# Neighbourhood attention of a fused four-block network: pairs of heads on TensorE side by side, values token-major

## The reference, cut to what matters

```
q = _heads(hx, w[:, :hd], na_q_g[j])            # RMS norm over each head
k = _heads(hx, w[:, hd:2 * hd], na_k_g[j])
v = _heads(hx, w[:, 2 * hd:])
k_c = _heads(hc, w[:, hd:2 * hd], na_k_g[j])    # 256 context tokens
v_c = _heads(hc, w[:, 2 * hd:])
...
    bias = jnp.take(bias_cols, row_off, axis=1)
    s_loc = jnp.einsum('bwhd,brwchd->bhwrc', q_r, k_win).astype(jnp.float32) * scale
...
x = x + gx1 * (_neighbourhood_attention(q, k, v, k_c, v_c, na_rpb[j]) @ na_w_out[j])
```

## Time and profile before

| | us |
|---|---|
| median of 3 runs | 3102.87 (3100.97 to 3104.98) |
| the profiled execution, its own time | 3100.61 |
| its span, first to last instruction | 3098.8 |
| from the start of `na_v` to the first turned numerators | 107.12 |
| the 64 attention steps | 153.28 |
| from the last of them to the first matmul of `res2` | 5.64 |
| PE busy, share of the span | 93% |
| granted TensorE clock, mean | 0.966 |

### The profile page before, as it was taken

The page is one execution under the profiler, slowest core; times in us unless marked ns, Lnnn a source line. Parts: engine busy times, 40 slices in busy tenths (PEclk is TensorE's granted clock), DMA queues, the critical chain, the costliest instruction groups (busy, mean ns, idle before and its releaser), DMA issues.

```text
span 3098.8 us, 39305 instructions
## 1 busy us (share of the span) xinstructions
PE 2885.5 (93%) x14018; PEld 2347.0 (76%) x14018; DVE 1626.7 (52%) x2371; ACT 1133.8 (37%) x1857; POOL 1090.1 (35%) x501
## 2 busy tenths in 40 slices
PE   4998899998998899997999799999979989989999
PEld 3885588886776578874878688888858878868887
DVE  6537696854456788855222416655542565431111
ACT  3333443334464533235112413121243357542222
POOL 2440444445322444443212123232323233234443
PEclk9999899998999899998999899999979989999999
DMA  5351355532421355531211123333312110122222
GB/s 209 122 181 34 119 187 203 190 109 79 158 69 65 108 185 193 178 109 42 68 68 48 41 82 115 130 133 121 126 61 67 50 42 22 36 76 98 95 95 88
DMA packets 90419, 325.47 MB, mean 105 GB/s; under 512 B 10036, under 2 KB 12852, under 8 KB 89784
## 3 DMA queue, kind: packets, MB, share of 16 engines
q1 hardware_dynamic: 85392, 312.21, 29.5%
q10 hardware_dynamic: 4904, 11.68, 1.2%
HBM read 321.75 MB, written 2.10 MB: 105 GB/s over the span
## 4 chain that ended last, share of the span: by engine, by line
PE 84%; DVE 8%; ACT 4%; issue 2%; DMA 1%; POOL 1%; DVEq 0%; ACTq 0%; SPq 0%; POOLq 0%
PE bank L1293 58%; PE junk L1295 9%; PE bank L1076 2%; PE bank L1221 2%; PE bank L1061 1%; PE bank L1208 1%; PE bank L1310 1%; PE bank L1200 1%; PE bank L1180 1%; PE junk L1200 1%; ACT UF L816 1%; ACT Uh L816 1%; PE bank L1102 1%; DVE ADA L1383 1%; DMA ADA<-in_ast 1%
## 5 line engine op out<-in xcount | busy, mean ns | idle before, releaser
L466 POOL TENSOR_TENSOR WL<-RAW,WH 128x1024 fp32r<-128x1024 f32 x392 | 979.1, 2499 | 1784.4 <-ACT WH L760 1276.7
L760 ACT ACTIVATE WH<-RAW 128x1024 fp32r<-128x1024 f32 x292 | 307.2, 1052 | 381.9 <-PE junk L1295 188.1
L1293 PE MATMUL bank<-U1h,WH 128*128 128x512 f32 x960 | 378.1, 394 | 18.0 <-DVE U1l L1631 17.8
L1293 PE MATMUL bank<-Uh,WH 128*128 128x512 f32 x832 | 341.2, 410 | 55.5 <-DVE Ul L1633 54.9
L1293 PE MATMUL bank<-U1l,WH 128*128 128x512 f32 x960 | 375.5, 391 | 0.0
L1293 PE MATMUL bank<-U1h,WL 128*128 128x512 f32 x960 | 375.4, 391 | 0.0
L1293 PE MATMUL bank<-Hh,WH 128*128 128x512 f32 x864 | 340.2, 394 | 11.7 <-DVE Hl L548 11.7
L1293 PE MATMUL bank<-Hl,WH 128*128 128x512 f32 x864 | 339.0, 392 | 0.0
L1293 PE MATMUL bank<-Hh,WL 128*128 128x512 f32 x864 | 338.8, 392 | 0.0
L1293 PE MATMUL bank<-Ul,WH 128*128 128x512 f32 x832 | 331.5, 398 | 0.0
L1293 PE MATMUL bank<-Uh,WL 128*128 128x512 f32 x832 | 331.2, 398 | 0.0
(11 more groups left out here) (334 smaller groups left out, 5249.3 us busy)
## 6 DMA issues: line engine op xcount, KB each, us to landing
RAW<-in_wst SPq DMA_DIRECT2D x392, 512.0 KB, 3.4
ADA<-in_ast SPq DMA_DIRECT2D x192, 512.0 KB, 4.5
NST<-in_nstrip ACTq DMA_DIRECT2D x16, 192.0 KB, 2.3
XT<-in_xt SPq DMA_DIRECT2D x1, 2048.0 KB, 15.4
STRIP<-in_strip ACTq DMA_DIRECT2D x8, 256.0 KB, 2.6
CB<-in_cb ACTq DMA_DIRECT2D x4, 512.0 KB, 4.2
DX<-in_dx ACTq DMA_DIRECT2D x1, 2048.0 KB, 8.3
out_xt<-XT SPq DMA_DIRECT2D x1, 2048.0 KB, 6.2
```

Source lines behind the costliest of these rows:

```text
L466: pool.tensor_tensor(WL[:, s4], RAW[:, s2], WH[:, s4].bitcast(F32), ALU.subtract)\
L760: act.activation(WH[:, c % 4], RAW[:, c % 2], ACT.Copy).then_inc(S("hi_done"), 1)
L1293: mm = pe.matmul(bank_of(p, u)[:], w[:, u, k], x[:, k, 0:T], start=st and m == 0, stop=en and m == 2)
```

## The change

1. Attention goes by pairs of heads: 32 steps i = 4t + b, for head pair t and query block b. Scores are three passes of two matmuls, head 2t from partitions 0 to 63 and head 2t+1 from 64 to 127, each 512 columns wide (256 context and 256 grid keys in one bank). Values are the stationary operand, 64 channels wide, and the turned numerators move: the two heads write partitions 0 to 63 and 64 to 127 of bank 4. The result has channels on partitions, so `turn_out` goes.
2. The division: the sums are spread over 64 columns each by a reciprocal into RB (`roots`), PE turns RB into bank 5 by eight f32 matmuls for each t (`spread`), ACT copies it to RX, DVE multiplies bank 4 by RX into OF (`out_of`), ACT and POOL split OF into OHN and OLN. The order of tokens changes there from grid columns to rows.
3. Masked biases come from memory, 768 KB for each t (`load_bias`), where POOL added mask and bias. Bias and maximum are one DVE instruction for each head (`na_logits`), 512 wide; ACT no longer copies context scores. Of the turned numerators ACT copies one head, DVE the other.
4. The high half of the keys is made by DVE (`key_hi`, was ACT).
5. The values are projected token-major (`na_values_pe`): tokens stationary, weights moving, 8 jobs in two halves of 512 channels, six banks for 768 tokens. `v_turn` goes; ACT and DVE copy three banks each at the end of a half, and two DMAs for each half make the copies of VN shifted by 64 tokens. The head norm of `na_k` tiles stays beside the jobs. The scores of step 0 are put ahead of the last bank's matmuls.
6. The norm ahead of the block writes its tokens by grid column (DVE, the branch k == 2), so ACT writes QN and KN without the reordering.

The diff, cut to its core (left out: POOL's loop that now only makes low halves, ACT's side with the same roles as described, layouts, semaphores' names, and the host's preparation):

```diff
-    add("na_v", 8, 3, "u", 48, ctx=True)
+    add("na_v", 8, 3, "u", 48)
...
+        NA_S = ((6, 7), (0, 1))
...
+                def low(t):
+                    pool.wait_ge(S("n_qhi"), t + 1)
+                    pool.wait_ge(S("n_khi"), t + 1)
+                    pool.tensor_tensor(QNl[:, t], QN[:, t], QNh[:, t % 2].bitcast(F32), ALU.subtract)
+                    pool.tensor_tensor(KNl[:, t * TC:(t + 1) * TC], KN[:, t], KNh[:, t % 2 * TC:(t % 2 + 1) * TC].bitcast(F32),
+                                       ALU.subtract).then_inc(S("n_lo"), 1)
+                def out_low(t):
+                    pool.wait_ge(S("o_hi"), 16 + t + 1)
+                    pool.tensor_tensor(OLN[:, t, 0:T], OF[:, t % 2], OHN[:, t].bitcast(F32), ALU.subtract).then_inc(S("o_ready"), 1)
+                pool.wait_ge(S("pe_job"), N_V + 5)
+                pool.memset(NB[:, 0:C], 0.0).then_inc(S("n_zero"), 1)
+                low(0)
+                for t in range(KT):
+                    if t + 1 < KT:
+                        low(t + 1)
+                    if t >= 1:
+                        out_low(t - 1)
...
+        def na_scores(pe, i):
+            t, b = divmod(i, 4)
+            if i >= 2:
+                pe.wait_ge(S("n_max"), 2 * i - 2)
+            elif i == 0:
+                pe.wait_ge(S("n_root"), 2 * KT)
+            else:
+                pe.wait_ge(S("nv_act"), 4)
+                pe.wait_ge(S("nv_dve"), 4)
+            if b == 0:
+                pe.wait_ge(S("n_lo"), t + 1)
+            q = slice(b * P, (b + 1) * P)
+            for m, (qs, ks) in enumerate(((QNh[:, t % 2], KNh[:, na_keys(t % 2, b)]), (QNh[:, t % 2], KNl[:, na_keys(t, b)]),
+                                          (QNl[:, t], KNh[:, na_keys(t % 2, b)]))):
+                for c in range(2):
+                    mm = pe.matmul(two(BANK[NA_S[i % 2][c]][:]), qs[64 * c:64 * c + 64, q], two(ks[64 * c:64 * c + 64]),
+                                   start=m == 0, stop=m == 2)
+            mm.then_inc(S("n_score"), 1)
+        def na_values_pe(pe, p, head_norm):
+            for j in range(8):
+                half, i = divmod(j, 4)
+                pe.wait_ge(S("lo_done"), N_V + j + 1)
+                for kk, b in ([(kk, b) for kk in range(2) for b in (0, 2, 5, 4, 1, 3)] if i < 3 else
+                              [(kk, b) for b in range(6) for kk in range(2)]):
+                    k = 2 * i + kk
+                    if j == 0 and (kk, b) == (0, 4):
+                        head_norm(1, phases[phases.index(p) - 1], 3)
+                        pe.wait_ge(S("n_root"), KT - 1)
+                    if (kk, b) == ((1, 5) if i < 3 else (0, 3)):
+                        head_norm(half, p, i)
+                    if j == 0 and kk == 0 and b < 4:
+                        pe.wait_ge(S("bank_read"), N_V - 1 + b % 2)
+                    if j == 7 and (kk, b) == (0, 5):
+                        na_scores(pe, 0)
+                    if half == 1 and k == 0:
+                        pe.wait_ge(S("nv_dve" if b % 2 else "nv_act"), b // 2 + 1)
+                    tok = slice(b * P, (b + 1) * P)
+                    for m, (x, w) in enumerate(((Uh, WH), (Ul, WH), (Uh, WL))):
+                        mm = pe.matmul(BANK[b][:], x[:, k, tok], flat(w[:, i, 4 * kk:4 * kk + 4]),
+                                       start=k == 0 and m == 0, stop=k == KT - 1 and m == 2)
+                    if k == KT - 1 and b < 5:
+                        mm.then_inc(S("nv_bank"), 1)
...
+            def turn(i):
+                for c in range(2):
+                    pe.wait_ge(S("n_exp"), 2 * i + c + 1)
+                    if i >= 1:
+                        pe.wait_ge(S("n_ptb" if c else "n_pta"), i)
+                    else:
+                        pe.wait_ge(S("nv_dve" if c else "nv_act"), 5)
+                    for s in range(4):
+                        mm = pe.transpose(BANK[2 + c][:, s * P:(s + 1) * P], ZP[:, i % 3, c, s * P:(s + 1) * P], IDENT[:])
+                    mm.then_inc(S("n_turned"), 1)
+            def av(i):
+                t, b = divmod(i, 4)
+                pe.wait_ge(S("n_pta"), i + 1)
+                pe.wait_ge(S("n_ptb"), i + 1)
+                if i == 0:
+                    pe.wait_ge(S("nv_act"), 6)
+                    pe.wait_ge(S("nv_dve"), 6)
+                elif b == 0:
+                    pe.wait_ge(S("n_of"), t)
+                if b == 1 and t % 4 == 0:
+                    pe.wait_ge(S("nv_shift"), 32 + 8 * t)
                 v0 = NA_VTILES.index(NA_KEY0[b])
                 v1 = NA_VTILES.index(NA_KEY0[b] + P)
-                for s, tile in enumerate((v0, v1, 7, 8)):
-                    mm = pe.matmul(BANK[6 + it % 2][:, 0:P], PTN[:, it % 2, s * P:(s + 1) * P], VN[:, tile, t * P:(t + 1) * P],
-                                   start=s == 0, stop=s == 3)
+                for s, tile in enumerate((7, 8, v0, v1)):
+                    for c in range(2):
+                        mm = pe.matmul(BANK[4][64 * c:64 * c + 64, b * P:(b + 1) * P],
+                                       VN[:, tile, (2 * t + c) * NHD:(2 * t + c + 1) * NHD],
+                                       PTN[:, i % 2, c, s * P:(s + 1) * P], start=s == 0, stop=s == 3)
                 mm.then_inc(S("n_av"), 1)
-            n = NH * 4
-            scores(0)
-            scores(1)
-            pe.wait_ge(S("vn_out"), 3 * KT)
-            for it in range(n):
-                if it + 2 < n:
-                    scores(it + 2)
-                turn(it)
-                if it >= 1:
-                    av(it - 1)
-            av(n - 1)
-            turn_out(pe, ON, lambda t, b: 64, "n_o", "n_back", (4, 5, 6, 7), "o_lo_na")
+            def spread(t):
+                pe.wait_ge(S("n_rb"), t + 1)
+                if t >= 1:
+                    pe.wait_ge(S("n_rx"), t)
+                else:
+                    pe.wait_ge(S("nv_dve"), 6)
+                for b in range(4):
+                    for c in range(2):
+                        mm = pe.matmul(BANK[5][64 * c:64 * c + 64, b * P:(b + 1) * P], RB[:, 2 * b + c], IDENT[:],
+                                       start=True, stop=True)
+                mm.then_inc(S("n_spread"), 1)
+            na_scores(pe, 1)
+            for i in range(NA_N):
+                if i + 2 < NA_N:
+                    na_scores(pe, i + 2)
+                if i % 4 == 0 and i:
+                    spread(i // 4 - 1)
+                turn(i)
+                if i >= 1:
+                    av(i - 1)
+            spread(KT - 1)
+            av(NA_N - 1)
...
-                    at_least(pe, S("vn_out"), 3 * jj)
-                    pe.wait_ge(S("n_root"), i * 4 + (8 + u + 1))
-                    starts = NA_VTILES + (T, T + P)
-                    for b, s0 in enumerate(starts):
-                        mm = pe.transpose(BANK[5 + b // 4][:, (b % 4) * P:(b % 4 + 1) * P], TT[:, u % 2, s0:s0 + P], IDENT[:])
...
+            def key_hi(t):
+                dve.wait_ge(S("n_scaled"), 8 + t + 1)
+                if t >= 2:
+                    dve.wait_ge(S("n_score"), 4 * (t - 1))
+                dve.tensor_copy(KNh[:, t % 2 * TC:(t % 2 + 1) * TC], KN[:, t]).then_inc(S("n_khi"), 1)
+            def values_dve(half, u):
+                head_norm_dve(half, u, 8)
+                if half == 1 and u == 1:
+                    for t in range(2):
+                        key_hi(t)
+                if u == 3:
+                    for b in (1, 3, 5):
+                        if half == 1 and b == 5:
+                            na_logits(0)
+                        nv_bank(dve, half, b)
+                        dve.tensor_copy(nv_tile(half, b), BANK[b][:]).then_inc(S("nv_dve"), 1)
+            def na_logits(i):
+                t, b = divmod(i, 4)
+                dve.wait_ge(S("n_score"), i + 1)
+                if b == 0:
+                    dve.wait_ge(S(f"nb_land{t % 2}"), 16 * (t // 2 + 1))
+                if i == 0:
+                    dve.wait_ge(S("n_zero"), 1)
+                if i >= 3:
+                    dve.wait_ge(S("n_turned"), 2 * i - 4)
+                for c in range(2):
+                    o = 2 * C * (1 + t % 2 * 6 + 3 * c + NA_MASK[b])
+                    m = 2 * (i % 3) + c
+                    dve.tensor_tensor_reduce(two(ZP[:, i % 3, c]), two(BANK[NA_S[i % 2][c]][:]), two(NB[:, 0:o]), -1.0, 3.0e38,
+                                             ALU.add, ALU.min, SM[:, m:m + 1]).then_inc(S("n_max"), 1)
...
+                    if k == 2:
+                        ins = dve.tensor_tensor(UF[:, t, 0:T].rearrange("p (w r) -> p r w", r=ROWS),
+                                                XT[:, t].rearrange("p (r w) -> p r w", r=ROWS),
+                                                RS[:, 0:T].rearrange("p (r w) -> p r w", r=ROWS), ALU.mult)
...
+                def roots(t):
+                    dve.wait_ge(S("n_exp"), 8 * t + 8)
+                    if t >= 1:
+                        dve.wait_ge(S("n_spread"), t)
```

(91 more changed lines are left out.)

281 lines of the change are left out of this document (96 added, 185 removed).

## The result

The changed kernel takes 3088.63 us (median of 7, 3076.77 to 3089.72), the kernel before beside it 3107.28 (median of 7). The ratio is 0.9928, interval 0.9908 to 0.9949: faster, by 18.7 us between the medians and some 22 by the ratio (which is not that of the medians), where 40.9 were forecast. 3088.6 lies outside the range of 3047 to 3086. The profiled execution took 3087.56 us, with a span of 3085.8.

A forecast was written before the change was run, and what follows sets the result against it. PE's own order was taken to bound the last block. Stretch ahead 86.7 + 3 clock, attention 131.3 + 3 clock, behind 0.1, norm 1: 225.1 against 266.0 us, 40.9 less, 3062 us; range 3047 to 3086.

The forecast's parts named there:

- the clock of the attention: Attention: waits of 2.3 us lower PE's clock a little, since 23% idle lies between two slices; 3 us added.
- The waits themselves: Attention: PE stands 2.3 us eight times before `spread` and 2.05 us six times before a new pair's scores.
- a clock under 0.9 in the attention: Sign named in advance that the forecast is wrong: a granted PE clock below 0.9 in the attention.
- the clock falls and stays low: Rival, attention: PE at clock 0.50 throughout, 195 us for 131, kernel 3123 us; chance 0.05.
- The column rival: Rival, attention: column halves don't overlap, eight value matmuls take 1.78 us instead of 0.89, kernel 3085 us; chance 0.14.
- The 2.38 times for three column tiles: Value matmuls in the attention: by this estimate eight take 1.13 us, not 0.89, and the kernel 3068 us.
- The waits are smaller: Rival: keys rounded in half the time, the norm costs nothing, the clock stays up; kernel 3052 us; chance 0.15.
- The width of a step: Attention: PE's own work is 12.8 us for each pair of heads, four steps, where it was 19.1.
- The wait in the middle of `na_v`: `na_v`, start of the second half: PE stands 3.6 us for the bank that DVE copies last.
- The whole stretch with its clock: Start of `na_v` to the first turn: 86.7 us plus 3 us for a clock lowered by waits.
- `nb_land`: Sign of a wrong forecast: an unnamed wait, above all for this; biases were expected well ahead, asked for 9 us before.
- The norm's write with a step of 32 bytes: Norm ahead of the block: DVE's strided write costs 0 to 0.5 us for each of 8 tiles; 1 us taken.

The follow-up runs named there:

- e5_front: e4_both plus: ACT copies all six value banks, PE starts the second half in that order, DVE's first logits moved ahead; 3026.1 us, ratio 0.9713.
- e4_both: Changed kernel with a reciprocal of 8 columns instead of 512 and queries and keys rounded two steps earlier; 3031.7 us, ratio 0.9760 to the kernel before.
- e1_fill: Changed kernel with superfluous PE transposes put before both waits of a pair of heads, no wait's cause made earlier; 3056.7 us, ratio 0.9844 to the kernel before.

## Why the prediction was wrong, point by point

**The step that failed is the clock of the attention**, "I add 3 us". It cost 21.6 us, the 122.49 busy us against the 100.90 of the same work without waits. The waits themselves were forecast rightly, and the sign that the prediction gave for being wrong, "a clock under 0.9 in the attention", came: 0.84. 40.9 forecast less 18.6 for this term is 22.3, and 22.1 was won. The others, a microsecond here and there, cancel.

The reasoning behind the 3 us compared idle shares of two slices of 10 us, "19% idle at 1.00" and "40% idle at 0.83", and put 23% between them. A share says nothing about how the idle time is divided. In the slice 940 to 950 of the kernel before, the timeline of PE has it in short pieces:

```profile
944.19 0.66 PE L1133 MATMUL junk<-IDENT,OD 128*128 128x128 f32 x4 [0.47 <-DVE OD L1753]
...
945.43 0.55 PE L1112 MATMUL bank<-IDENT,PD 128*128 128x128 f32 x3 [0.17 <-DVE PD L1740]
...
947.69 0.47 PE L1091 MATMUL junk<-OH,WH 128*128 128x512 f32 x1 [1.26 <-issue]
```

And some 30 us later the same timeline held nearly my case, waits of 2.2 us behind a busy stretch:

```profile
977.80 0.66 PE L1133 MATMUL bank<-IDENT,OD 128*128 128x128 f32 x4 [2.20 <-DVE OD L1753]
980.69 0.80 PE L1091 MATMUL bank<-OH,WH 128*128 128x512 f32 x1 [2.23 <-DVE OL L1766]
981.28 0.63 PE L1091 MATMUL bank<-OL,WH 128*128 128x512 f32 x1
981.71 0.63 PE L1091 MATMUL bank<-OH,WL 128*128 128x512 f32 x1
...
985.55 0.63 PE L1091 MATMUL junk<-OH,WL 128*128 128x512 f32 x1
```

There PE stood twice for 2.2 us. The four transposes behind the first take 0.66 us, as at full clock, but the twelve matmuls of 512 columns behind the second stand 0.43 us apart and not 0.23: 2.4 us lost. Had I taken even half of that, 1.2 us, for each of fourteen waits, it had been 17 us for the 3, and the forecast 3076. The prediction chose its yardsticks by their idle share, and not by the length of the single wait.

**The rivals.** That the clock falls and stays low, 3123 us, did not come: it rises again within the pair. But its place was right, "the idle pieces before each spread and each new pair", and its condition, "a mean clock of about 0.6", was too coarse; the truth lies between it and the forecast. The Trainium skill, "TensorE: Matmul & The Clock Gate", section "HAM oscillation — how this bites in real kernels", describes this pattern: a kernel that waits in every round of its loop and begins every round at half clock. The trace agrees with the pattern for thirteen of the fourteen waits; the 21.6 us are 1.5 for each of the fourteen. The column rival is refuted: sixteen records in 1.09 us. The 2.38 times for three column tiles, which the Trainium skill, "TensorE: Matmul & The Clock Gate", section "Measured speedup vs the span model", states, carried over as an estimate to 1.13 us for eight value matmuls, is not borne out for two: they take 0.89 and the end of the last. "The waits are smaller" is refuted: they are 31.9 us where 30.7 were worked out.

**What held.** The width of a step: PE's work in the attention is 100.9, forecast 100.6. The wait in the middle of `na_v`: 3.5 us before PE L1274, ended by DVE VN L1697, forecast 3.6 in that place. The whole stretch with its clock: 89.1, forecast 89.7, though in part by luck. PE's busy time in it is 82.25 us, and 80.07 in `e5_front` at full clock, where 65.4 + 11.2 and two sets of scores, 78.4, were worked out. So the work is 1.7 us more, the clock 2.2 for 3, and PE stands 6.9 where the sum leaves 8.3: three misses that cancel. `res2` follows the last value matmuls without idle time, forecast 0.1. `nb_land` is in no wait.

**Terms off in size without effect.** These DVE groups are of the changed kernel (busy us, mean ns, idle before):

```profile
L1771 DVE TENSOR_TENSOR UF<-XT,RS 128x512 f32<-128x512 f32 x8 | 8.8, 1095 | 0.0
L1941 DVE TENSOR_TENSOR OF<-bank,RX 128x512 f32<-128x512 f32 x8 | 9.3, 1164 | 6.2 <-PE bank L1308 6.2
L1684 DVE CAST KNh<-KN 128x768 fp32r<-128x768 f32 x6 | 3.3, 556 | 0.0
```

The norm's write with a step of 32 bytes costs 0.4 us more than the 0.69 of a plain one, inside the bounds of 0 to 0.5, and the norm to the start of `na_v` is not longer for it (145.7 us, 146.5 before): the 1 us that I took does not show. OF reads and writes in another order and takes 1.16 us, where I had 0.69 from a plain row; the rounding of the keys takes 0.56 where I had 0.85. The two sit in the same wait and nearly cancel, which is why 2.1 us came out where 2.05 was forecast.

## What to carry to other kernels

Price each wait on PE with what follows it: look in the trace for single idle pieces as long as the one that a change will make, more than one, and read the starts of the matmuls behind them; an idle share of a window, or a mean clock, can't tell that. Where a wait of this kind can't be removed, matmuls that write what is overwritten next are enough to win back what the clock takes (21 us here), and in the one run of it filling the wait half way did as well. Before that, look at what is waited for: here one reciprocal of 512 columns that held eight different numbers, and a rounding issued two steps late, were worth 53 us.

## What the runs showed of the hardware that was not expected

- A stationary operand can be one column read 64 times, at no price: `spread` takes 1.09 us for it in `e4_both`, as it does from 64 stored columns at full clock in `e1_fill`.
- With PE never idle and a granted clock of 1.00, the same 300 us held 1733 matmuls in one execution and 1700 in another of the same kernel.
- PE's clock stayed at 1.00 through an attention with 12% standing time in pieces of up to 1.9 us, and was 0.84 in one with 21% in pieces of up to 3.0. A wait of the same 2.1 to 3.0 us mostly has half clock behind it, but not always: in 25 of 28 cases in the two profiles of the changed kernel.
